# Three late pairs of down-projection tiles: other slots, another queue, another spread of rows

## The reference

```python
def swiglu(x, w1, w3, w2):
    return (jax.nn.silu(x @ w1) * (x @ w3)) @ w2

    top_logit, top_idx = lax.top_k(logits, TOP_K)
    gates = jax.nn.softmax(top_logit, axis=-1)
    ...
    # each expert's tokens through swiglu(xb, w1[e], w3[e], w2[e]), D_FF = 2816
    # times their gates, added to x; then rms_norm(x, final_norm)
```

## Time and profile before

| | us |
|---|---|
| median of 3 runs (lowest, highest) | 1150.67 (1150.56, 1152.05) |
| the profiled execution | 1152.23 |
| its span, first to last instruction | 1149.6 |
| PE busy | 1132.8 (99%) |
| DVE, ACT, POOL busy | 420.3, 162.7, 34.7 |
| read from HBM | 348.71 MB, 305 GB/s over the span |

### The profile page before, as it was taken

The page is one execution under the profiler, slowest core; times in us unless marked ns, Lnnn a source line. Parts: engine busy times, 40 slices in busy tenths (PEclk is TensorE's granted clock), DMA queues, the critical chain, the costliest instruction groups (busy, mean ns, idle before and its releaser), DMA issues.

```text
span 1149.6 us, 26766 instructions
## 1 busy us (share of the span) xinstructions
PE 1132.8 (99%) x12153; PEld 742.8 (65%) x12153; DVE 420.3 (37%) x926; ACT 162.7 (14%) x354; POOL 34.7 (3%) x34
## 2 busy tenths in 40 slices
PE   9999999999999999999999999999999999999995
PEld 7889889999999889874455334574444434444441
DVE  5756668787455384433121110210212022021012
ACT  4416212100100035322000000000000000000011
POOL 0013000000000000000110000100100000000000
PEclk9999999999999999999999999999999999999999
DMA  9800054453534338669999999999999999999995
GB/s 341 317 1 2 4 219 174 166 200 150 202 149 160 152 122 341 271 246 397 394 423 424 423 426 424 423 424 425 422 426 423 425 423 427 420 426 422 426 408 204
DMA packets 50104, 352.10 MB, mean 306 GB/s; under 512 B 4844, under 2 KB 10488, under 8 KB 20160
## 3 DMA queue, kind: packets, MB, share of 16 engines
q1 hardware_dynamic: 48384, 347.26, 74.1%
q0 software_dynamic: 1152, 2.90, 0.6%
q10 hardware_dynamic: 448, 0.17, 0.1%
HBM read 348.71 MB, written 2.11 MB: 305 GB/s over the span
## 4 chain that ended last, share of the span: by engine, by line
PE 95%; DMA 2%; DVE 1%; ACT 0%; issue 0%; DVEq 0%; SPq 0%
PE ps L692 95%; DMA x<-in_moe 1%; DMA W<-in_ffn 1%; PE ps L762 0%; DVE xn L2405 0%; PE ps L1128 0%; ACT S L1705 0%; PE ps L1166 0%; DVE W L1968 0%; DVE W L1970 0%; DVE S L1886 0%; ACT S L1470 0%; DVE W L1915 0%; DVE xn L2332 0%; DVEq L115 0%
## 5 line engine op out<-in xcount | busy, mean ns | idle before, releaser
L692 PE MATMUL ps<-W,S 128*32 128x352 f32 (+4 forms) x6216 | 490.9, 464 | 1.4 <-ACT W L1651 0.8
L692 PEld LDWEIGHTS ps<-W,S 128*32 128x32 f32 (+2 forms) x6216 | 225.2, 111 | 254.5 <-issue 229.4
L692 PE MATMUL ps<-xn,W 128*128 128x256 f32 (+2 forms) x1232 | 222.9, 339 | 0.0
L692 PEld LDWEIGHTS ps<-xn,W 128*128 128x128 f32 (+1 forms) x1232 | 195.8, 190 | 22.7 <-issue 2.7
L692 PE MATMUL ps<-S,W 128*128 128x128 f32 (+3 forms) x1552 | 202.8, 290 | 1.5 <-DVE x L2059 0.7
L692 PEld LDWEIGHTS ps<-S,W 128*128 128x128 f32 (+2 forms) x1552 | 190.1, 190 | 9.2 <-issue 1.7
L2347 DVE TENSOR_TENSOR S<-S,ps 128x352 f32<-128x352 f32 x42 | 21.9, 521 | 421.4 <-ACT S L1643 418.7
L692 PE MATMUL ps<-S 128*32 128x512 f32 (+5 forms) x1502 | 126.1, 467 | 3.9 <-DMA S<-in_moe 2.5
L692 PEld LDWEIGHTS ps<-S 128*32 128x32 f32 (+2 forms) x1502 | 54.2, 115 | 69.2 <-issue 53.4
L1643 ACT ACTIVATE S<-ps 128x352 f32<-128x352 f32 x42 | 17.7, 462 | 545.2 <-PE ps L692 542.9
L692 PE MATMUL ps<-W 64*64 64x64 f32 (+2 forms) x1080 | 48.0, 231 | 0.5 <-DVE W L1904 0.4
(11 more groups left out here) (329 smaller groups left out, 563.1 us busy)
## 6 DMA issues: line engine op xcount, KB each, us to landing
W<-in_moe SPq DMA_DIRECT2D x116, 1408.0 KB, 29.4
W<-in_moe SPq DMA_DIRECT2D x44, 1024.0 KB, 29.9
S<-in_moe SPq DMA_DIRECT2D x33, 1024.0 KB, 29.6
W<-in_ffn SPq DMA_DIRECT2D x11, 2048.0 KB, 8.3
S<-in_moe SPq DMA_DIRECT2D x12, 1408.0 KB
W<-in_ffn SPq DMA_DIRECT2D x4, 2816.0 KB, 11.0
x<-in_moe SPq DMA_DIRECT2D x11, 1024.0 KB, 29.3
W<-in_l_w_in SPq DMA_DIRECT2D x4, 2048.0 KB, 20.0
```

What stands on the lines that cost most here:

```text
L692: return nc.tensor.matmul(o, l, r, start=start, stop=stop, **kw)
```

## The change

Pairs 85, 86 and 87 no longer use pair slots. They go to unit slots that are not needed again: those of units 118, 119 and 121 (`LATE`). Pair 85 is still requested by SyncE, right behind pair 84, after a wait for unit 118. Pairs 86 and 87 (`TURNED`, places 9 and 10 of the expert) are requested by GpSimd after its gathers, each after a wait for its unit. Each is two DMAs: rows 0 to 7, and rows 8 to 127 as eight groups of 15. The 120 rows are stored in another order in DRAM (`moe2t`, made on the host), so that the rows of one group lie 8 rows apart. Both add to one semaphore, on which TensorE waits for 32. In passes after the first, the counts of the shared semaphores and one wait are adapted.

```diff
+TURNED = (9, 10)
...
+        LATE = {PAIRED - 3: UNITS - USLOTS, PAIRED - 2: UNITS - USLOTS + 1, PAIRED - 1: UNITS - USLOTS + 3}
...
+        in_turned, TURNED0 = (g_in, pool_io), (gins(E - 1), 16 * CH)
...
             def load_d(n, v):
                 p, i = divmod(v, NB)
                 src = chosen_rows(u2, p, i, NB) if p else u2[v]
+                if n == 0 and v in LATE:
+                    room = unit_slot(0, LATE[v])
+                    sp.dma_start(slots[room][:, 0:2 * D], src).then_inc(in_u[room], 16)
+                    return
...
-                for pair in range(NB * (E - 1) - DSLOTS, PAIRED - DSLOTS):
+                for pair in range(NB * (E - 1) - DSLOTS, PAIRED - DSLOTS - len(LATE)):
                     refill_down(0, pair)
+                for v in sorted(LATE):
+                    if v - NB * (E - 1) not in TURNED:
+                        sp.wait_ge(m_u, LATE[v] + 1)
+                        load_d(0, v)
                 sp.wait_ge(m_u, LAST + 1)
...
             for e in range(1, E):
                 gather(e)
+            turned_pairs = A["moe2t"].rearrange("(u p) n -> u p n", p=P)
+            pool.wait_ge(flag_done, 1)
+            last_expert = pool.value_load(chosen_expert[0:1, E - 1:E], min_val=1, max_val=E - 1)
+            for i, p in enumerate(TURNED):
+                v = NB * (E - 1) + p
+                room = unit_slot(0, LATE[v])
+                at = pool.snap(last_expert * len(TURNED) + i, min_val=len(TURNED), max_val=E * len(TURNED) - 1)
+                src = turned_pairs[bass.ds(at, 1)].rearrange("u p n -> (u p) n")
+                pool.wait_ge(m_u, LATE[v] + 1)
+                pool.dma_start(slots[room][0:8, 0:2 * D], src[0:8, :]).then_inc(in_turned[i], 16)
+                pool.dma_start(slots[room][8:P, 0:2 * D], src[8:P, :].rearrange("(b a) n -> a b n", a=8)).then_inc(in_turned[i], 16)
...
-                pe.wait_ge(in_d[pair_slot(n, v)], pair_in(n, v))
-                w2p = w2t[pair_slot(n, v)].rearrange("p (u n) -> p u n", u=2)
+                if n == 0 and v in LATE:
+                    if p in TURNED:
+                        i = TURNED.index(p)
+                        pe.wait_ge(in_turned[i], TURNED0[i] + 32)
+                    else:
+                        pe.wait_ge(in_u[unit_slot(0, LATE[v])], unit_in(0, LATE[v]) + 16)
+                    w2p = slots[unit_slot(0, LATE[v])][:, 0:2 * D].rearrange("p (u n) -> p u n", u=2)
+                else:
+                    pe.wait_ge(in_d[pair_slot(n, v)], pair_in(n, v))
+                    w2p = w2t[pair_slot(n, v)].rearrange("p (u n) -> p u n", u=2)
...
+    w2 = o["moe2"].reshape(E, NB, P, 2 * D)[:, list(TURNED)]
+    rest = w2[:, :, 8:].reshape(E, len(TURNED), 8, 15, 2 * D).transpose(0, 1, 3, 2, 4).reshape(E, len(TURNED), P - 8, 2 * D)
+    o["moe2t"] = np.ascontiguousarray(np.concatenate([w2[:, :, :8], rest], 2)).reshape(E * len(TURNED) * P, 2 * D)
```

More of the change, by code:

```diff
@@ L404, in unit_in @@
                 before += len([v for v in range(UNITS) if unit_slot(m, v) == s])
+            if n:
+                before += len([v for v in LATE if v - NB * (E - 1) not in TURNED and unit_slot(0, LATE[v]) == s])
             return 16 * (before + u // (OVER_SLOTS if n else USLOTS) + 1)
@@ L413, in pair_in @@
             for m in range(n):
-                before += len([i for i in range(PAIRED) if pair_slot(m, i) == s])
+                before += len([i for i in range(PAIRED) if pair_slot(m, i) == s and not (m == 0 and i in LATE)])
             return 16 * (before + v // (OVER_PAIRS if n else DSLOTS) + 1)
@@ L631, in _ @@
                     sp.wait_ge(m_u, UNITS * n)
+                    sp.wait_ge(m_d, PAIRED * n)
                     for i in range(OVER_SLOTS):
                         load_u(n, i)
-                    sp.wait_ge(m_d, NB * E * n)
                     for v in range(OVER_PAIRS):
```

## The result

The changed kernel takes 1167.44 us (median of 4 runs, 1167.21 to 1167.72) against 1150.62 for the kernel before in the same session: ratio 1.0141, 95% interval 1.0129 to 1.0153, or 16.8 us slower. The forecast was 1149.8 with a range up to 1159.5. The profiled execution took 1167.21 us, its span is 1165.2.

What follows compares the result with a forecast made beforehand. The prediction took a lagging half of the saturated DMA engines to bound the kernel's end. Late engines relieved of 4.3 us, with two pairs' products (3.43 us) exposed, left 0.85 us saved: 1149.8 us, whole range 1147.6 to 1159.5.

Steps and rivals of the forecast that it cites:

- What bounds the kernel: At the last expert's down pairs, eight DMA engines lag by 7 to 8 us; waits cost TensorE 4.48 us.
- Slots, earlier requests, GpSimd's idle time: New slots and pair 85's request about 14 us earlier cost and gain nothing; GpSimd's issues fit idle time.
- Who carries the rows: For pairs 86 and 87, late engines carry 2 rows instead of 16, saving 4.3 us; early ones carry 30.
- The row against the step: Store evidence for the rival that the place written sets pace: 1154.1 to 1159.7 us, named 1157, chance 0.23.
- the rule as the prediction used it: GpSimd's cursor moves on over consecutive engines, so the 8-row and 120-row DMAs take complementary halves.
- Units and earlier pairs: Before pair 85, a late engine loses 0.6 us, delaying only waits for pairs 83 to 85; units cause no wait.
- The sum: Pair 85 starts at 1132.85, pair 87 2 x 1.715 us later at 1136.28 against 1137.13: 0.85 us saved.
- The sign by which it was to be known: First rival, place written sets pace (0.23): software-queue packets of 0.4 us or more, waits from pair 77 on.
- wrong half: Rival: late engines carry the 120 rows of each turned pair, +7.7 us, 1158.4; chance 0.10.
- all sixteen: Rival: GpSimd spreads the 120 rows over all engines, 8 each; +3.4 to +3.9 us, 1154.3; chance 0.10.

Runs made afterwards that it cites:

- the plain run: Changed kernel, but GpSimd requests pairs 86 and 87 whole, one DMA of 128 rows each: 1154.92 us, ratio 1.0029 against the kernel before.
- SyncE alone: Changed kernel without the GpSimd block, all three pairs requested whole by SyncE into the late slots: 1151.87 us against 1151.45 for the kernel before.
- the sixteen groups: Changed kernel, but GpSimd requests pairs 86 and 87 each as one DMA of sixteen groups of 8 rows: 1164.68 us, ratio 1.0113 against the kernel before.
- the probe: Kernel before plus one SyncE request of 8 rows of 64 B behind pair 84, to see which engines carry it: 1151.89 us in one run.

## Why the prediction was wrong, point by point

**What bounds the kernel**: right. In the plain run pair 85 started at 1137.14, when the late engines had carried everything. One reading was loose: in the earlier trace rows the digits are 9 from the nineteenth slice on, not from the sixteenth; nothing hangs on it.

**Slots, earlier requests, GpSimd's idle time**: right. With SyncE alone the ratio is 1.000. GpSimd's four issues took 0.57, 0.69, 0.52 and 0.64 us, and its waits held nothing up.

**"Who carries the rows"**: this step failed. It took 14 rows x 0.31 us from each late engine and gave them to each early one at the same 0.31 us, as if an engine's time were all that a row costs. The runs show that an 8 KB row took 0.55 us and not 0.31 on both queues, and that this goes with which engine writes which partitions. The Trainium skill ("SBUF — State Buffer", on the DMA port swizzle) says that the rate of a DMA depends on how many of 16 ports its partitions reach, and that partitions 0 to 63 reach half of them. The traces agree in part: cut the usual way, 128 rows run at 423 GB/s, and cut into halves of 64 partitions at 249 to 305. But the sixteen groups write all 128 partitions in one transfer and still ran at 272 to 284, so the number of ports reached isn't all of it. The row against the step was in the prediction, 76 ns against 48 for a row of 1 KB, and I gave it 0.23.

The same step took it that both long transfers fall on the half that is ahead. They fell on different sets of eight, as the 43.8% of GpSimd's queue shows; the rule as the prediction used it, by which each transfer moves on by eight engines, is not borne out. So each engine carried 15 rows by the one or the other, about the 16 of before, and no late engine was relieved. Even without any contention the 4.3 us could not have come. Two neat halves that a transfer can address are doubtful as well: the eight engines of the probe, on SyncE's queue, are a mixture of six and two.

**Units and earlier pairs**: failed with it. I let a late engine lose 0.6 us. The last four units waited 10.5 us in all, because the engines moved 15 GB/s each in place of 26.3, also those that had no turned row: up to 1105 us only eight engines had any, and yet none of SyncE's 167 unit packets from 1094 to 1105 took less than 0.53 us.

**The sum**: the term of products exposed behind pair 85, 2 x 1.715 us, is right; the plain run measures 3.5 us. The relief of 4.3 us did not come, and 12.2 us of lost transfer took its place: 12.16 + 3.46 = 15.6 us between the two profiled executions' last products.

The sign by which it was to be known, software-queue packets over 0.4 us and early waits, was right, except that the first wait came at unit 124, not at pair 77.

**The rivals "wrong half" and "all sixteen"**: neither happened. A long transfer used eight engines, a quarter of the sixteen's time and not half, and the two used different ones.

**What stays open.** Why eight engines lag: the sum of instruction packets fits (64 us over eight engines), but no run changed them. How the late engines are spread over the two sets of eight that GpSimd's transfers use. Whether fewer than two engines on one place would be free: no run tried a group that fits the usual cut. A version that beats both kernels was not found; all that leave every row in its usual place end with the late engines, and the best of them equals the kernel before.

## What to carry to other kernels

When transfers saturate the DMA engines, keep each row with the engine that a whole 128-partition transfer gives it: another cut of the same bytes, even one that gives every engine the same rows, can take 40% of the rate of everything in flight. Read GB/s beside the DMA share, since the share stays at 1.0 when engines wait for one another. And a transfer moved ahead of its turn delays what it passes: products whose data is early are worth nothing if they stand behind the one that is last.

## What the runs showed of the hardware that I had not expected

- Two plain DMAs of 64 rows instead of one of 128, with contiguous rows and the same queue, cost 9.0 us on two 1 MB tiles beside a saturated stream (12.5 us over the kernel before against 3.5) and slowed all of it to 249 to 305 GB/s.
- Rows 64 KB apart in DRAM cost nothing: 420 to 431 GB/s.
- TensorE's granted clock falls while it waits: 0.75 and 0.68 in 1110 to 1122 us of the changed kernel, where it waited 6.5 us for unit 125. These are means over windows in which it stood partly at 1.2 GHz (0.5) and partly at 2.4 GHz (1.0). Units then take 4.92 and 4.27 us, not 2.57. It cost nothing there, as transfers set the end; in the run with sixteen groups the clock was 0.74 from 1146 to 1152 and lengthened products that wait for nothing. The first two below take 5.28 us from start to start, not 3.43, so about 1.8 us of that run's time is the clock:

```profile
1144.48 2.46 PE L715 MATMUL ps<-S 128*32 128x512 f32 x16 [2.05 <-DMA S<-in_moe]
1146.95 2.98 PE L715 MATMUL ps<-W,S 128*32 128x512 f32 x16
1149.76 1.89 PE L715 MATMUL ps<-S 128*32 128x512 f32 x16
```

- A slow stretch on the engines reaches SyncE: an issue behind a full queue took 6.92 us for pair 84 in the changed kernel (2.76 in the earlier trace rows).
